# Transposes of the probabilities alternated with projection matmuls, and ScalarE's second copy moved behind the exponential, in a decoder block's mixers

## The reference

```
h = rms_norm(x);  proj = h @ w_in        # split into q, k, v of two mixers, forget gates, two output gates
forgetting attention, 8 heads of 64:     s = q k^T / 8 + F_q - F_k, causal;  p = softmax(s);  o = p v
dilated attention, 12 heads of 64:       windows (128, 512, 2048) at dilations (1, 4, 16), 4 heads each,
                                         mixed by the softmax of their log-sum-exp
x = x + (sigmoid(ga) * (oa @ w_a) + sigmoid(gb) * (ob @ w_b)) @ w_out
x = x + square(relu(rms_norm(x) @ w_up)) @ w_down;   y = rms_norm(x)
```

## Time and profile before

| | before |
|---|---|
| median of three runs | 1581.77 us (1577.9 to 1582.29) |
| profiled execution | 1580.75 us, span 1578.9 us |
| TensorE matmul busy | 1508.9 us, 96% of the span |
| TensorE weight load busy | 1242.5 us |
| VectorE busy | 1094.0 us |
| ScalarE busy | 797.1 us |
| transposes, L1185 | x428, 73.2 us, mean 273 ns |
| projections in the mixers, L1131 | x1536, 422.5 us, mean 408 ns |
| ScalarE copies, L1650 (work) | x144, 51.4 us, mean 369 ns |

### The profile page before, as it was taken

One profiled execution on the slowest core, in us unless ns is written; L12 is line 12 of the kernel. 1 busy time (PEld: TensorE's weight loads), 2 busy tenths in 40 slices (PEclk: granted clock), 3 DMA queues, 4 the chain that ended last, 5 costly groups with the idle time before them and its releaser, 6 DMA issues. The chain is left out here.

```text
span 1578.9 us, 20832 instructions
## 1 busy us (share of the span) xinstructions
PE 1508.9 (96%) x7364; PEld 1242.5 (79%) x7364; DVE 1094.0 (69%) x1747; ACT 797.1 (50%) x1438; POOL 9.5 (1%) x24
## 2 busy tenths in 40 slices
PE   6999999998999999999999999999999899999997
PEld 5788887886888888788888878888888677777776
DVE  5687777755756768843665676666666887777776
ACT  5577666653767775534224453343334444444442
POOL 1000000000000000000000000000000000000001
PEclk9999999999999999999999999999999999999999
DMA  5321111111022113333635424444446664444402
GB/s 187 95 67 28 41 54 41 31 38 27 19 63 68 28 41 91 97 107 107 214 120 160 134 86 150 165 151 149 147 147 210 236 226 147 147 147 147 147 27 107
DMA packets 168277, 173.40 MB, mean 110 GB/s; under 512 B 7848, under 2 KB 127720, under 8 KB 167792
## 3 DMA queue, kind: packets, MB, share of 16 engines
q1 hardware_dynamic: 168176, 172.07, 33.9%
HBM read 125.84 MB, written 46.20 MB: 109 GB/s over the span
## 5 line engine op out<-in xcount | busy, mean ns | idle before, releaser
L1131 PE MATMUL ps<-hspl,wsp 128*128 128x512 f32 x1536 | 422.5, 408 | 6.6 <-ACT tmp L1572 3.1
L1131 PEld LDWEIGHTS ps<-hspl,wsp 128*128 128x128 f32 x1536 | 265.0, 189 | 53.1 <-ACT tmp L1572 5.8
L1483 PE MATMUL ps<-dn_b,a_hi 128*128 128x512 f32 x896 | 280.1, 394 | 18.7 <-DVE keep L2328 13.1
L1483 PEld LDWEIGHTS ps<-dn_b,a_hi 128*128 128x128 f32 x896 | 168.2, 190 | 61.1 <-issue 22.9
L1483 PE MATMUL ps<-dn_b,a_lo 128*128 128x512 f32 x448 | 175.8, 392 | 0.0
L2328 DVE TENSOR_TENSOR keep<-keep,ps 128x512 f32<-128x512 f32 (+1 forms) x144 | 101.6, 713 | 41.7 <-PE ps L1483 23.4
L1483 PE MATMUL ps<-up_b,a_hi 128*128 128x512 f32 x384 | 118.5, 390 | 0.6 <-DVE up_b L2328 0.6
L1944 ACT ACTIVATE keep<-keep 128x512 f32<-128x512 f32 x64 | 40.5, 633 | 125.6 <-DVE keep L2630 42.0
L1483 PEld LDWEIGHTS ps<-dn_b,a_lo 128*128 128x128 f32 x448 | 84.8, 189 | 17.9
L2328 DVE TENSOR_TENSOR dn_b<-dn_raw,dn_b 128x1024 fp32r<-128x1024 f32 x56 | 67.1, 1221 | 39.4 <-ACT dn_b L1960 39.4
L2215 DVE TENSOR_TENSOR keep<-ps,o_part 64x256 f32<-64x256 f32 x80 | 39.7, 496 | 76.8 <-ACT o_part L1665 76.3
(11 more groups left out here) (242 smaller groups left out, 2823.9 us busy)
## 6 DMA issues: line engine op xcount, KB each, us to landing
hidden<-keep SPq DMA_DIRECT2D x112, 256.0 KB, 2.2
dn_raw<-hidden SPq DMA_DIRECT2D x56, 512.0 KB, 6.1
raw<-in_w_in SPq DMA_DIRECT2D x35, 512.0 KB, 3.7
a_raw<-in_w_up SPq DMA_DIRECT2D x36, 256.0 KB, 3.1
sgl<-sg SPq DMA_DIRECT2D x8, 1024.0 KB, 5.1
a_raw<-in_w_down SPq DMA_DIRECT2D x32, 256.0 KB, 3.1
spare<-in_w_down SPq DMA_DIRECT2D x32, 256.0 KB, 3.9
spare<-in_w_up SPq DMA_DIRECT2D x28, 256.0 KB, 3.2
```

What stands on the lines that cost most here:

```text
L1131: ins = pe.matmul(psp(u, g), wsp[c % 2][:, wp, k * P:(k + 1) * P], hspl[:, mp, k, cols], start=(n == 0), stop=(n == 23), skip_group_check= ...
L1483: ins = pe.matmul(o, a_part(n, j, wp, k), b_block(n, j, mp, k), start=(first and k == 0 and m == 0), stop=(k == ks - 1 and m == 2), skip_g ...
```

## The change

Two edits. On TensorE, the share of projection matmuls is no longer issued in thirds: after the first third, one projection matmul follows each transpose, as long as the step's share has any, and what is left follows the last transpose. On ScalarE, `probs_hi` is called once for each unit: the first unit as before ahead of `exps`, the second, where there is one, behind `exps` and ahead of the casts. Nothing else differs; the number and the operands of all instructions are the same, and VectorE's list is untouched.

```
--- before.py
+++ after.py
@@ -1133,15 +1133,16 @@
                 if b == 24:
                     ins.then_inc(w_used if g % 2 else half_done, 1)
 
-            def project_part(G, part):
+            def share(G):
 
                 t, s = divmod(G, STEPS)
-                if t < MIX:
-                    for u, g, steps in group_steps(t):
-                        if s in steps:
-                            per = 24 // len(steps)
-                            a = (s - steps[0]) * per
-                            project(u, g, a + per * part // 3, a + per * (part + 1) // 3)
+                return [(u, g, 24 // len(steps), s - steps[0]) for u, g, steps in group_steps(t) if s in steps]
+
+            def project_next(G, a, b):
+
+                for u, g, per, n in share(G):
+                    if a < min(b, per):
+                        project(u, g, n * per + a, n * per + min(b, per))
 
             def scores(G):
                 t, s = divmod(G, STEPS)
@@ -1174,7 +1175,8 @@
                         ins = pe.matmul(oo, lt, rh, start=(m == 0), stop=(m == len(ops) - 1), skip_group_check=True)
                 ins.then_inc(qk_done, 1)
 
-            def transposes(G):
+            def transposes(G, ahead, more):
+
                 pe.wait_ge(exp_done, G + 1)
                 if G % STEPS == 1:
                     pe.wait_ge(v_lo, 2 * (G // STEPS) + 2)
@@ -1184,7 +1186,12 @@
                     for k in range(a, b):
                         ins = pe.transpose(PS[2][:, (u % 2) * HALF + (k - a) * P:(u % 2) * HALF + (k - a + 1) * P],
                                            probs(G)[:, k * P:(k + 1) * P], ident[:])
-                    ins.then_inc(tr_done, 1)
+                        if k == b - 1:
+                            ins.then_inc(tr_done, 1)
+                        if more:
+                            project_next(G + 1, ahead, ahead + 1)
+                            ahead += 1
+                return ahead
 
             def inverse_rows(f):
 
@@ -1220,14 +1227,13 @@
                 for G in range(first, last + 2):
                     if G < last:
                         scores(G)
+                    ahead = sum(per // 3 for _, _, per, _ in share(G)) if G < last else 0
                     if G < last:
-                        project_part(G, 0)
+                        project_next(G, 0, ahead)
                     if first <= G - 1 < last:
-                        transposes(G - 1)
+                        ahead = transposes(G - 1, ahead, G < last)
                     if G < last:
-                        project_part(G, 1)
-                    if G < last:
-                        project_part(G, 2)
+                        project_next(G, ahead, 24)
                     if G % 2 and first <= G - 3 < last:
                         if G % STEPS == 1 and first and G < last:
                             inverse_rows(G // STEPS - N_DIL - 1)
@@ -1640,10 +1646,11 @@
                 act.activation(probs(G)[:, 0:n * P], psc[G % 2][:, 0:n * P], ACT.Exp,
                                bias=stat(G, 0), scale=-1.0, accum_out=stat(G, 1)).then_inc(exp_done, 1)
 
-            def probs_hi(G):
-                if G // 2 == BLOCKS * N_DIL + 1:
+            def probs_hi(G, n):
+
+                if n == 0 and G // 2 == BLOCKS * N_DIL + 1:
                     act.wait_ge(comb_ok, 4)
-                for n, (a, b) in enumerate(units_of(G)):
+                for a, b in units_of(G)[n:n + 1]:
                     u = units_before(G) + n
                     act.wait_ge(tr_done, u + 1)
                     after(act, pv_done, G // 2 - 1)
@@ -1677,9 +1684,12 @@
                     if G < last and G // 2 + 1 < BLOCKS * MIX:
                         query_hi(G // 2 + 1, G % 2)
                     if first <= G - 1 < last:
-                        probs_hi(G - 1)
+                        probs_hi(G - 1, 0)
                     if G < last:
                         exps(G)
+                    if first <= G - 1 < last:
+                        probs_hi(G - 1, 1)
+                    if G < last:
                         if s == 1:
                             values_hi(t)
                         if t < N_DIL:
```

## The result

The changed kernel takes 1593.23 us in the median of nine runs (1585.45 to 1596.9), against 1582.4 us of nine runs before. The ratio is 1.0069, with a 95% interval of 1.0053 to 1.0084: 10.8 us slower.

A forecast was written before the change was run, and what follows sets the result against it. TensorE's own stream was taken to bound the kernel. Stalls of 2.1 + 1.1 + 3.1 + 0.7 = 7.0 us, nothing removed, on the profiled 1580.75 gave 1587.8, stated as 1588.5; forecast 1585 to 1593 (0.55), 8-in-10 range 1581 to 1596.

The forecast's parts named there:

- Price of one transpose (part 1): TensorE's order: a transpose costs 0.11 us alone or in a block, so 223 alternations cost and save 0.
- rival B: The long matmul hides the transpose's weight load: 0.05 saved per gap, 11 us, against 7 lost; 1578; chance 0.06.
- ScalarE's data 0.69 later (part 2): First bank of four transposes, three projections between them, complete 0.69 us later; the swap gives back 0.34 with eight tiles.
- step 9: Its start in the first three forgetting heads: evacuation chain 0.69 us later each, 2.1 us in all.
- Dilated steps at nothing: Dilated steps, one bank of at most two transposes, 0.23 us late: costed at nothing, VectorE's max releasing most exponentials.
- Step 12: First and last forgetting heads: evacuation 0.9 us late against 0.5 and 0.2 of cover; 0.4 and 0.7, 1.1 us.
- Step 0: Start of the next head, behind steps 14 and 15: late chain through VectorE's max and evacuation; stalls of 1.2 and 1.4 us.
- The 0.5 at the transposes of step 14, second head: In the next head, a further ScalarE cast in the chain: 0.5 us of stall at the transposes.
- Small stalls: Forgetting mixer: up to 0.1 us in even seven-tile steps and a few short steps of three or four tiles; 0.7 us.
- Rival A: The slack holds: only step 9's 2.1 us and some 1 us more stay; 1584, not measurable; chance 0.27.
- Rival C: A wait takes over in every two-bank step: 0.4 us in most of 32, 13 us plus 2.1; 1597; chance 0.10.
- Rival D: The change does not do what it says, shares having no projections left; time as before, 1582; chance 0.02.

The follow-up runs named there:

- Experiment 4: Against the kernel before: alternation in the dilated heads only, ScalarE's order as before; 1580.17 us, ratio 0.999.
- experiment 5: Against the changed kernel: only a second bank's transposes alternated, the first bank's in a block, swap kept; 1582.43 us, ratio 1.0003 to the kernel before.
- 6: Against the kernel before: alternation only in one-bank steps (up to four tiles), all heads, ScalarE's order as before; 1584.24 us, ratio 1.0014.
- experiment 3: Against the changed kernel: both edits, but alternation in the forgetting heads only; 1592.04 us, ratio 1.0072 to the kernel before.
- 9: The changed kernel run again with no edit; 1589.93 us, ratio 1.0056 to the kernel before.
- 10: Changed kernel, evacuation ahead of the cast behind step 8 of the second and third forgetting heads; 1588.69 us, ratio 1.0043 to the kernel before.
- 12: Changed kernel, evacuation ahead of the casts behind step 8 (two forgetting heads), step 2's projections all ahead of the transposes; 1581.83 us, ratio 0.9999 to before.
- experiment 1: Against the changed kernel: ScalarE's calls back in the order of before, alternation alone; 1590.87 us, ratio 1.0062 to the kernel before.
- experiment 8: Against the kernel before: all of step 2's projections ahead of the transposes of step 1 in each head; 1576.23 us, ratio 0.9963.

## Why the prediction was right, and where its sizes were off

The direction and the mechanism held: 1588.5 was forecast, 1581 to 1596 as the range, and 1593.23 was measured. By its own steps:

- **Price of one transpose (part 1), taken as 0: right.** The ends in the alternation move by 0.11 and 0.23 to 0.24. Experiment 4 has 44 changes at no cost; experiment 5 has 45 with +1.1 us of mixer, where the swap alone has +1.2. The 11 us of rival B never appeared. The Trainium skill ("TensorE: Matmul & The Clock Gate", section "LDWEIGHTS (loading the stationary operand)") has a formula for the time of a weight load, which gives 107 ns for 128 columns, an estimate. That is close to the 0.11 us that a transpose costs here with a long matmul on either side; the runs show this distance and not what makes it.
- **ScalarE's data 0.69 later (part 2): right.** The copy came 0.71 later behind the first transpose. Experiments 5 and 6 show from both sides that the first bank's lateness carries step 9. Dilated steps at nothing: right.
- **Step 9, 2.1 us: right to a tenth.** Idle time 0.85 to 1.54 in the second head, 1.12 to 1.80 in the third, none to 0.60 in the first: 2.0.
- **Step 12, 1.1 us: too much.** By the ends of the instructions, some 0.35 us in two heads. In the first head the evacuation came 1.01 later (419.94 against 418.93) and TensorE's scores of that step 0.32 later (419.46 against 419.14), so 0.7 of delay and not 0.9. In the last head TensorE had waited 0.7 at the transposes ahead of it and found cover, which the sum did not carry along.
- **Step 0, 1.2 and 1.4 us: the mechanism right, the size well over.** Idle time 0.46 and 0.62 (0.7 and 0.9 by the starts of the scores). It was not cover that TensorE had gained: it began step 14 0.7 us later than before (427.41 against 426.73) and step 0 as much later (435.75 against 435.03), which moves the chain and its consumer alike. With this 0.7 taken off, the last max began at 432.5 where 432.9 was forecast, and the evacuation ended at 435.9 where 436.5 was. The links were taken a little too long: the exponential of step 14 began 0.49 behind the start of the copy and not 0.62, and the second copy and the evacuation took 0.96 together and not 1.1.
- **The 0.5 at the transposes of step 14, second head: right size, wrong releaser.** And one like it, in the last head, was missed. Timeline of the changed kernel: ScalarE's exponential of step 10, VectorE's subtractions of the two banks of step 9, and the transposes of step 10.

```profile
590.88 0.79 ACT L1646 ACTIVATE tmp<-ps,fox_stat 128x640 f32<-128x640 f32 x1 [0.32 <-DVE fox_stat L2204]
...
591.36 1.12 DVE L2211 TENSOR_TENSOR work<-ps,work 128x512 fp32r<-128x512 f32 x2
...
592.19 0.30 PE L1187 MATMUL ps<-ident,tmp 128*128 128x128 f32 x1 [0.53 <-DVE work L2211]
```

The transposes may not write their bank before VectorE has subtracted what lay there two units ago, at about 592.05. Part 2 looked only at the exponential. The subtraction is late because ScalarE's copy is, and VectorE has run the max and a weight remainder ahead of it. Idle time 0.53 (0.7 by the ends), against the tenth that the sum had.
- **Small stalls, 0.7 us: too little**, about 1.6 in many places of 0.1 to 0.3 and one of 0.4 behind the last scores.

The whole can be read without any sum: take the first start of the scores in each step (line 1174 before, 1175 after). The 63 steps from the first to the last scores of the forgetting mixer are 6.6 us longer, and from the last scores to the last values matmuls (599.95 to 607.61 before, 606.05 to 614.12 after) it is 0.4 more: 7.0 us of stalls, of which step 9 has 2.1, step 0 1.6, the transposes of step 14 in the second head 0.7 and those of step 10 in the last 0.7. That this is the 7.0 of the forecast is in part luck: steps 12 and 0 were taken some 1.8 too dear, and what was missed or too small at the transposes and in small stalls came to as much. The mixer is 8.0 us longer; the last 1.0 is a half-clock episode at 614.8 us: the last values matmuls, up to the first gate matmul, take 2.90 us and not 1.94.

**The term that was missing is the granted clock.** The forecast treated it as given, since the earlier trace rows has 1.00 in both mixers. Two views of TensorE by stretch, the changed kernel first, then before; the value behind the busy time is the granted clock:

```profile
610.00:620.00 10.00, 8.37 (x48) 0.83 0.00 0
630.00:640.00 10.00, 10.00 (x46) 1.00 0.78 210
650.00:660.00 10.00, 7.88 (x28) 0.83 0.48 131
```

```profile
610.00:620.00 10.00, 10.00 (x46) 1.00 0.49 158
630.00:640.00 10.00, 8.18 (x30) 0.83 0.26 105
650.00:660.00 10.00, 10.00 (x46) 1.00 0.05 7
```

The changed kernel has an episode at the end of the forgetting mixer (615 us) and one at 656; before has one at 636. Among the fourteen profiles, the five with both edits in the forgetting heads (the changed kernel, 3, 9, 10, 12) all have two episodes between 600 and 700 us; the other nine have one or none. Over all runs, the time goes with the mean clock: the runs of before reach from 1576.05 us at 0.997 to 1585.95 at 0.991, and a straight line through all 63 gives 1.3 us for each 0.001. The 0.002 between the means of before and of the changed kernel is then some 2.6 us, by this estimate. So of 10.5 us, the difference of the two means of all runs, 7.0 are the stalls, some 2.6 go with the clock (the episode in the mixer is part of that), and about 1 us is not accounted for. That the alternation and the swap together bring on the extra episodes is argued from five profiles against nine, and from experiment 1, whose mean clock stayed at 0.994 with more stalls (9.2 us in the mixer, 9.6 in the time, so there the stalls account for nearly all of it); what in them does it is open. It also explains the profiled execution: with 0.995 it had the best clock of its nine runs.

Rival A (the slack holds) fell: only step 9 and two small places had none, but the chains reached steps 0 and 12 as well, through VectorE at step 0. Rival C fell too: waits in a few of the 32 two-bank steps, not in most. Rival D: 223 alternations are there.

## What to carry to other kernels

When an engine at its limit interleaves filler work into a block whose result others wait for, the filler is free in throughput and is paid for as latency: price it by the slack of every consumer down the queue, the third and fourth too, and count each delay against the consumer's own start, since a stall ahead of both moves both and is no cover. Leave whole what the next engine needs first, and put filler only where the profile shows a stall to fill; here ten stalls of 1 us stood beside the transposes, and moving six projections there, with one evacuation ahead of a cast, gave 5 to 6 us, while alternating cost 9 to 11. Removing a stall shows what it covered: of the 9 to 11 us expected of experiment 8, half came back elsewhere.

## What was not expected of the hardware

The granted clock falls for short stretches close behind some of TensorE's waits, so a wait may cost more than its length. Of the half-clock episodes in the profiles of before, the changed kernel, 3 and 6, 20 of 25 began within 10 us of the start of an idle gap of more than 1.5 us on TensorE. It is not shown that the gap brings the episode on: of the 39 such gaps behind the kernel's start 19 had none within that time. Step 9 of the third forgetting head has a gap of 1.8 us, then an episode at 533 us in experiment 3 and at 529 in 6; in the changed kernel the same gap brought none. The episode at 614.8 us in the changed kernel stands behind a gap of 1.56 us, and before has the same gap at that place with no episode.

The values matmuls of 256 columns at that place in the changed kernel began 0.12 us apart ahead of the episode and 0.21 to 0.22 in it:

```profile
614.58 0.28 PE L1213 MATMUL ps<-work 128*128 128x256 f32 x1
614.70 0.28 PE L1213 MATMUL ps<-pt_odd,work 128*128 128x256 f32 x1
...
615.42 0.41 PE L1213 MATMUL ps<-pt_odd,work 128*128 128x256 f32 x1
615.64 0.41 PE L1213 MATMUL ps<-work 128*128 128x256 f32 x1
```

The mean granted clock of a run spread from 0.991 to 0.998 on the kernel before alone, and its time by 10 us, more than most edits here are worth.
